# Weighting of matches shared by ScalarE and GpSimd, and four buffers of raw expert rows, in a decoder block with product-key experts

## What is computed

```python
idx = i_top0 * PEER_NKEYS + i_top1            # 8 x 16 experts of a token
act = gelu(einsum("phkd,pd->phk", u_tab[idx], tb))
out = einsum("phk,phkd->pd", g * act, v_tab[idx])
```

## Time and profile before

| | |
|---|---|
| median of 3 runs | 2198.37 us (2197.58 to 2199.71) |
| profiled execution | 2195.7 us |
| its span, first to last instruction | 2193.9 us |
| granted TensorE clock, mean | 0.981 |
| TensorE / VectorE / ScalarE / GpSimd busy | 94% / 80% / 37% / 36% of the span |
| first table with spreading | 1097 to 1613 us |
| rest of the first table | 1613 to 1655 us |
| second table | 1655 to 2182 us |

### The profile page before, as it was taken

One profiled execution on the slowest core, in us unless ns is written; L12 is line 12 of the kernel. 1 busy time (PEld: TensorE's weight loads), 2 busy tenths in 40 slices (PEclk: granted clock), 3 DMA queues, 4 the chain that ended last, 5 costly groups with the idle time before them and its releaser, 6 DMA issues. The chain is left out here.

```text
span 2193.9 us, 35121 instructions
## 1 busy us (share of the span) xinstructions
PE 2069.3 (94%) x11175; PEld 1812.6 (83%) x11175; DVE 1748.5 (80%) x3357; ACT 816.6 (37%) x1350; POOL 798.8 (36%) x673
## 2 busy tenths in 40 slices
PE   6998988979999998999899999999999999999997
PEld 5886788758888877889799999999997888888886
DVE  3776655677768845999799999999988888888887
ACT  4454423522322223344443443344333333333333
POOL 2000044500000000325488989888963222222221
PEclk9999999989999999999999999999999999999999
DMA  6743100405234215224489999999899999999995
GB/s 136 93 61 39 20 1 20 135 13 139 70 91 117 79 62 178 68 73 153 143 284 300 325 333 320 318 323 322 278 362 373 338 337 337 338 337 336 341 335 198
DMA packets 296052, 445.77 MB, mean 203 GB/s; under 512 B 84612, under 2 KB 221988, under 8 KB 295716
## 3 DMA queue, kind: packets, MB, share of 16 engines
q1 hardware_dynamic: 239348, 273.26, 41.9%
q0 software_dynamic: 41472, 151.01, 19.7%
q10 hardware_dynamic: 15152, 20.51, 2.5%
HBM read 398.05 MB, written 46.14 MB: 202 GB/s over the span
## 5 line engine op out<-in xcount | busy, mean ns | idle before, releaser
L2278 PE MATMUL bank<-u_hi,u_one 128*128 128x512 f32 x768 | 299.7, 390 | 3.6 <-DVE u_two L2426 3.6
L2278 PE MATMUL bank<-u_lo,u_one 128*128 128x512 f32 x768 | 299.3, 390 | 0.0
L2278 PE MATMUL bank<-u_hi,u_two 128*128 128x512 f32 x768 | 299.2, 390 | 0.0
L2261 PE MATMUL bank<-xt_hi,u_hi 128*128 128x352 f32 x832 | 277.9, 334 | 0.7 <-DVE u_lo L2316 0.7
L1997 POOL DMA_INDIRECT row_slot<-in_peer_v_dram,row_index x128 | 141.1, 1102 | 377.1 <-DVE row_x L2434 362.6
L2261 PE MATMUL bank<-xt_lo,u_hi 128*128 128x352 f32 x832 | 269.1, 323 | 0.0
L2261 PE MATMUL bank<-xt_hi,u_lo 128*128 128x352 f32 x832 | 268.9, 323 | 0.0
L2499 ACT ACTIVATE u_hi<-xh 128x1024 fp32r<-128x1024 f32 x128 | 135.8, 1061 | 334.9 <-PE bank L2278 331.4
L2423 DVE TENSOR_TENSOR u_lo<-xh,u_hi 128x1024 fp32r<-128x1024 f32 x128 | 156.9, 1226 | 81.2 <-ACT u_hi L2499 81.1
L2190 POOL TENSOR_TENSOR u_two<-u_match,u_weight_hi 128x512 fp32r<-128x512 f32 x96 | 179.9, 1874 | 31.2 <-DVE u_match L2324 30.5
L1517 PE MATMUL bank<-xt_hi,x_whi 128*128 128x512 f32 x448 | 177.8, 397 | 1.6 <-DVE xt_lo L181 0.9
(11 more groups left out here) (464 smaller groups left out, 5024.7 us busy)
## 6 DMA issues: line engine op xcount, KB each, us to landing
xh<-in_peer_v_dram SPq DMA_DIRECT2D x128, 512.0 KB, 5.5
xh<-in_peer_u_dram SPq DMA_DIRECT2D x104, 512.0 KB, 6.3
x_raw<-in_w_in_dram SPq DMA_DIRECT2D x56, 512.0 KB, 6.9
acts<-xh ACTq DMA_DIRECT2D x102, 192.0 KB, 5.2
weights<-u_spread SPq DMA_DIRECT2D x32, 512.0 KB, 9.8
v_gg<-weights SPq DMA_DIRECT2D x128, 128.0 KB, 5.3
p_raw<-in_w_in_dram SPq DMA_DIRECT2D x12, 1024.0 KB, 10.0
q_raw<-in_peer_u_dram SPq DMA_DIRECT2D x24, 512.0 KB, 3.7
```

Source lines behind the costliest of these rows:

```text
L2261: mm = pe.matmul(k.ps[4 + b][:, 0:DOTTED], w[b][:, c, :], x[:, c, 0:DOTTED], start=(c == 0 and w is uhi and x is hi), stop=(c == DC - 1 an ...
L2278: mm = pe.matmul(k.ps[q][:, :], h[b][:, t * P:(t + 1) * P], w[b][:, f], start=start and h is hhi and w is vhi, stop=stop and h is hlo, ski ...
```

## The change

- GpSimd's `weigh` makes the low product only, counted by a new semaphore `low_done`. A new `weigh` on ScalarE makes the high product, as four copies of 128x128 with a scale per partition, for step s+1, between the high parts of tile s+1 and the Gelu of tile s. The weight tiles are four columns wider, so that a step behind the last has zeros.
- VectorE's two comparisons are parted: `matches` comes first in the step, ahead of the low parts, and waits for both products of the step before; `onehot` stays where it was.
- Raw rows have four buffers: two in `xh`, and the first two quarters of the residual's tile. Load i+4 waits until tile i is turned. The other two quarters of the residual are loaded at i = 96 as before, the first two after the last loads of the second table; the additions wait for them.
- Pieces of a chunk are stored in iterations 1, 2, 4, 6, 8, 10, 12 and 13 of the next chunk, not 0, 2, ... 14.
- ScalarE waits for the split of the gathered weights at the start of the last chunk.
- In the second table the first loads into `xh` 2 and 3 wait for one turn less.

```diff
@@ -1980,6 +1980,7 @@
+STORE_AT = (1, 2, 4, 6, 8, 10, 12, 13)
@@ -2015,15 +2016,16 @@
-        raw = [k.xh[:, 2 + b, :] for b in range(2)]
 ...
-        weight_hi = k.sb("u_weight_hi", [P, DENSE], F32R, ctx=st)
-        weight_lo = k.sb("u_weight_lo", [P, DENSE], ctx=st)
+        weight_hi = k.sb("u_weight_hi", [P, DENSE + TOK_TILE], F32R, ctx=st)
+        weight_lo = k.sb("u_weight_lo", [P, DENSE + TOK_TILE], ctx=st)
 ...
-        names = ("raw_in", "turned", "hi_done", "lo_done", "product", "ga_done", "ga_out")
+        raw_in = k.sems("u_raw_in", PER)
+        low_done = k.sem("u_low_done")
+        names = ("turned", "hi_done", "lo_done", "product", "ga_done", "ga_out")
@@ -2073,11 +2075,12 @@
-        last_ga = [match[:, :, :].rearrange("p q n -> p (q n)")[:, 0:DENSE], weight_lo[:, :]]
+        last_ga = [match[:, :, :].rearrange("p q n -> p (q n)")[:, 0:DENSE], weight_lo[:, 0:DENSE]]
 ...
+        raw = [k.xh[:, 2, :], k.xh[:, 3, :], rest[:, 0, :], rest[:, 1, :]]
@@ -2101,12 +2104,11 @@
-                def load(n, u):
-
-                    b, before = place(n, u)
-                    sp.wait_ge(s["turned"][b], after(before * 2))
-                    sp.dma_start(raw[b], u_dram[:, bass.ds((n * PER + (u + EARLY)) % EXPERT_TILES, 1), :].rearrange("p a d -> p (a d)")
-                                 ).then_inc(s["raw_in"][b], 16)
+                def load(i):
+
+                    if i >= PER:
+                        sp.wait_ge(s["turned"][i % 2], after((i - PER) // 2 * 2 + 2))
+                    sp.dma_start(raw[i % PER], u_dram[:, (i + EARLY) % EXPERT_TILES, :]).then_inc(raw_in[i % PER], 16)
@@ -2123,14 +2125,16 @@
+                for i in range(2, PER):
+                    load(i)
                 for i in range(tiles):
-                    if i + 2 < tiles:
-                        load(i // PER, i % PER + 2)
-                    c, piece = i // CHUNK_STEPS - 1, i % CHUNK_STEPS // 2
-                    if 0 <= c < STORED and i % 2 == 0:
-                        store(c, piece)
+                    if i + PER < tiles:
+                        load(i + PER)
+                    c, at = i // CHUNK_STEPS - 1, i % CHUNK_STEPS
+                    if 0 <= c < STORED and at in STORE_AT:
+                        store(c, STORE_AT.index(at))
                     if i == steps:
-                        sp.dma_start(rest[:, :, :], residual).then_inc(res_in, 16)
+                        sp.dma_start(rest[:, 2:TT, :], residual[:, 2:TT, :]).then_inc(res_in, 16)
@@ -2148,7 +2152,7 @@
-                        sp.wait_ge(s["turned"][u - 2], after(2 * uses))
+                        sp.wait_ge(s["turned"][u - 2], after(2 * uses - 2))
@@ -2166,6 +2170,9 @@
+                for b in range(2):
+                    sp.wait_ge(s["turned"][b], after(2 * uses))
+                sp.dma_start(rest[:, 0:2, :], residual[:, 0:2, :]).then_inc(res_in, 16)
@@ -2186,9 +2193,8 @@
-                    for h, part in enumerate((weight_hi[:, tok].bitcast(F32), weight_lo[:, tok])):
-                        pool.tensor_tensor(two[b][:, :, h, :], match[:, :, :], part.unsqueeze(2).to_broadcast([P, TOK_TILE, P]),
-                                           ALU.mult).then_inc(two_done, 1)
+                    pool.tensor_tensor(two[b][:, :, 1, :], match[:, :, :], weight_lo[:, tok].unsqueeze(2).to_broadcast([P, TOK_TILE, P]),
+                                       ALU.mult).then_inc(low_done, 1)
@@ -2235,16 +2241,17 @@
-                    pe.wait_ge(s["raw_in"][b], after(before * 16))
+                    pe.wait_ge(raw_in[u % PER], after((n + u // PER) * 16 + (16 if u % PER >= 2 else 0)))
 ...
-                            mm = pe.transpose(k.ps[2 * b + f][:, c % 4 * P:(c % 4 + 1) * P], raw[b][:, c * P:(c + 1) * P], k.ident[:, :])
+                            mm = pe.transpose(k.ps[2 * b + f][:, c % 4 * P:(c % 4 + 1) * P], raw[u % PER][:, c * P:(c + 1) * P], k.ident[:, :])
 ...
-                    pe.wait_ge(two_done, after(step * 2 + 2))
+                    pe.wait_ge(two_done, after(step + 1))
+                    pe.wait_ge(low_done, after(step + 1))
@@ -2316,12 +2323,15 @@
-                def onehots(at, b):
-
-                    keys = k.row[:, :].unsqueeze(1).to_broadcast([P, TOK_TILE, P])
-                    picks = lambda n: chosen[:, n, at].unsqueeze(2).to_broadcast([P, TOK_TILE, P])
-                    dve.tensor_tensor(one[b][:, :, :], keys, picks(0), ALU.is_equal).then_inc(one_done, 1)
-                    dve.tensor_tensor(match[:, :, :], keys, picks(1), ALU.is_equal).then_inc(match_done, 1)
+                keys = k.row[:, :].unsqueeze(1).to_broadcast([P, TOK_TILE, P])
+
+                def onehot(at, b):
+                    dve.tensor_tensor(one[b][:, :, :], keys, chosen[:, 0, at].unsqueeze(2).to_broadcast([P, TOK_TILE, P]), ALU.is_equal
+                                      ).then_inc(one_done, 1)
+
+                def matches(at):
+                    dve.tensor_tensor(match[:, :, :], keys, chosen[:, 1, at].unsqueeze(2).to_broadcast([P, TOK_TILE, P]), ALU.is_equal
+                                      ).then_inc(match_done, 1)
@@ -2358,19 +2368,23 @@
+                        if c is not None:
+                            step = n * PER + u
+                            dve.wait_ge(two_done, after(step + 1))
+                            dve.wait_ge(low_done, after(step + 1))
+                            matches(bass.ds(step * TOK_TILE + TOK_TILE, TOK_TILE))
 ...
-                            step = n * PER + u
                             dve.wait_ge(spread_ready, after(step))
-                            dve.wait_ge(two_done, after(step * 2 + 2))
-                            onehots(bass.ds(step * TOK_TILE + TOK_TILE, TOK_TILE), (u + 1) % 2)
+                            onehot(bass.ds(step * TOK_TILE + TOK_TILE, TOK_TILE), (u + 1) % 2)
 ...
-                        dve.wait_ge(two_done, after(2 * steps))
+                        dve.wait_ge(two_done, after(steps + 1))
+                        dve.wait_ge(low_done, after(steps))
@@ -2382,13 +2396,15 @@
-                dve.tensor_copy(weight_hi[:, :], chosen[:, 2, 0:DENSE]).then_inc(weight_split, 1)
+                dve.memset(chosen[:, :, DENSE:DENSE + TOK_TILE], 0.0).then_inc(weight_split, 1)
                 dve.wait_ge(weight_split, after(1))
-                dve.tensor_tensor(weight_lo[:, :], chosen[:, 2, 0:DENSE], weight_hi[:, :].bitcast(F32), ALU.subtract).then_inc(weight_split, 1)
-                dve.memset(chosen[:, :, DENSE:DENSE + TOK_TILE], 0.0).then_inc(weight_split, 1)
+                dve.tensor_copy(weight_hi[:, :], chosen[:, 2, :]).then_inc(weight_split, 1)
+                dve.wait_ge(weight_split, after(2))
+                dve.tensor_tensor(weight_lo[:, :], chosen[:, 2, :], weight_hi[:, :].bitcast(F32), ALU.subtract).then_inc(weight_split, 1)
 ...
-                onehots(slice(0, TOK_TILE), 0)
+                matches(slice(0, TOK_TILE))
+                onehot(slice(0, TOK_TILE), 0)
@@ -2448,6 +2464,7 @@
+                    dve.wait_ge(res_in, 32 if t < 2 else 16)
@@ -2485,6 +2502,15 @@
+                def weigh(step, b):
+                    act.wait_ge(match_done, after(step + 1))
+                    act.wait_ge(spread_ready, after(step - 1) if not isinstance(step, int) else max(step, 1))
+                    for q in range(TOK_TILE):
+                        at = bass.ds(step * TOK_TILE + q, 1) if not isinstance(step, int) else slice(step * TOK_TILE + q, step * TOK_TILE + q + 1)
+                        for h, part in ((0, weight_hi[:, at].bitcast(F32)),):
+                            ins = act.activation(two[b][:, q, h, :], match[:, q, :], ACT.Copy, scale=part)
+                    ins.then_inc(two_done, 1)
+
@@ -2507,13 +2533,14 @@
+                        if c is not None:
+                            weigh(n * PER + (u + 1), (u + 1) % 2)
 ...
-                            act.wait_ge(match_done, after(steps + 1))
-                            act.wait_ge(two_done, after(2 * steps))
+                            act.wait_ge(two_done, after(steps + 1))
@@ -2527,10 +2554,14 @@
+                    if c == CHUNKS - 1:
+                        act.wait_ge(weight_split, after(5))
 ...
+                act.wait_ge(weight_split, after(3))
+                weigh(0, 0)
 ...
```

## The result

| | before | after |
|---|---|---|
| median of the runs | 2198.61 us (4 runs, 2197.58 to 2199.71) | **2176.47 us** (4 runs, 2173.27 to 2178.45) |
| ratio to before | | 0.9898, 95% interval 0.9881 to 0.9915 |
| profiled execution, its span | 2195.7, 2193.9 | 2176.06, 2174.3 |
| mean granted clock | 0.981 | 0.981 |

Two runs further down that took 2954.83 and 4205.35 us, where all others of their kernels lie within 6 us, are left out of every number.

A forecast was written before the change was run, and what follows sets the result against it. GpSimd's multiplications and late loads were taken to hold the expert-tile stage above TensorE's pace. Stage -25.9, start -1.0 and end of tiles -1.9 sum to -28.8 us, from 2198.4 to 2169.6; range 2164 to 2184.

The forecast's parts named there:

- The stage on TensorE's pace: Expert-tile stage: GpSimd's multiplications and late loads cost 26.4 us over TensorE's own pace; the change saves 25.9 there.
- the floor of 5.154: Expert-tile stage: us per spread step when TensorE has nothing to wait for, against 5.43 before.
- the change takes no work from TensorE: Expert-tile stage: TensorE's work stays the same, so the 26.4 us lost to something else is the whole prize.
- the second table is otherwise untouched: Second-table stage: the same instruction by instruction, with no term in the sum.
- 6.9 with waits: GpSimd in the expert-tile stage: about 6.9 us stay per two steps, down from 10.68, against 10.31 on TensorE.
- 9.6 us per two steps forecast: VectorE in the expert-tile stage: falls from 10.43 us to 9.6 per two steps, against 10.31 on TensorE.
- The 0.84: VectorE per two steps: 0.84 us of a dot product and GpSimd's multiplication excluding each other, claimed to go.
- rival B: Expert-tile stage: GpSimd's low multiplication meets VectorE's dots every step, 5.64 us each, total 2215.5 us; chance 0.06.
- Loads: Raw expert tiles: four buffers and later stores together remove the transposes' load waits, 23.0 us in 12 places.
- Start, last chunk, end of the tiles: Around the stage: start -1.0 us, ScalarE's wait for weights at the last chunk +0.5, eight tiles without spread -1.9.
- A: Transfers bind and load waits stay: 2181.1 us if half of the 23.0 stays, 2192.6 if all; chance 0.12.
- C: ScalarE bounds the stage, by copies at 0.74 us or a late wait for matches: 2193, at half 2181; chance 0.06.

## Why the prediction was right, and where it was short

**The stage on TensorE's pace: right.** Chain on TensorE alone (from 1300 to 1345 us), no wait on a load and dots of 1.21 to 1.23 us throughout the stage. With the operands' distance kept, the floor of 5.154 is met to a nanosecond (5.153), and the whole kernel takes 2168.5 us against the 2169.6 forecast. That the kernel as it was changed lands in the range too, 6.9 us above the forecast, is in part luck: its range had no room set aside for what follows, and 32 bytes instead of 64 would have put it far outside.

**The step that failed: "the change takes no work from TensorE" and "the second table is otherwise untouched".** The instructions are, their operands' places aren't. Two tiles four columns wider move u_hi and u_lo by 64 bytes, and each product on them costs 1% more: 4.1 us in the second table, 4.0 in the stage, some 0.3 in the eight tiles behind it. I read the diff for its instructions and not for the layout behind a widened tile. No row of before could have given the price, but that a tile moved was to be seen.

**GpSimd: right.** It has 271.37 us of work in 493, 5.7 us per two steps where I had put 6.9 with waits.

**ScalarE: right.** I took 368 ns for a copy; one takes 391 on average, but they overlap, so that four in a row are 1.28 us against 1.5. The estimate from the Trainium skill (ScalarE: Activation LUTs, What ACT_TABLE_LOAD costs) was 1.2; the trace agrees. The work is hidden: the wait ahead of the Gelu is 0.96 us a step still. How well it hides depends on the order of VectorE's work, which I had priced only by the exclusion.

**VectorE: 9.6 us per two steps forecast, 10.24 measured** (486.72 us in the 490 us of the kernel with old distances, 95.1 steps). The 0.84 did go from the dots, and 0.67 came back on the one-hot: its mean is 1028 ns in the stage, 692 before. This is the wider rule of the Trainium skill (SBUF — State Buffer, Who interferes with whom), by which a comparison with both inputs in SBUF is excluded too; the trace agrees (0.68 us alone, 1.40 beside GpSimd). So the step "the 0.84 goes too, and VectorE falls to 9.6" did not hold: one hit in two steps stayed, as rival B has it. It cost nothing only because 10.24 is just under TensorE's 10.31. I had left 0.7 us of room and 0.07 is left, and that it was enough is luck.

**Loads: right.** The prediction says that GpSimd's lag and the load waits overlap, and takes both at once. The trace shows the overlap: the weighting alone brings the load waits from 25.8 to 11.0 us. By medians the stores alone give 5.9 us, stores with buffers 11.4, the weighting alone 20.0, and all of it 28.3; the sum of the last two parts, 31.4, is 3.1 more than the whole, which is not clear of the noise. What I had as two parts that act "together" need not both be there: the four buffers alone would have done.

**Start, last chunk, end of the tiles.** From the transposes of the two tiles turned ahead of the stage to the stage's first ones it is 10.34 us after, 11.21 before: -0.9 against -1.0. The new wait at the last chunk is there (2.0 us, once), but no transposes come late by it: 0 instead of 0.5. The end gained 2.7 us instead of 1.9; the wait for the first weighted tile is 2.48 us, 0.24 shorter, the rest came from between the tiles.

**The rivals.** Of A nothing: with a DMA share of 0.98 in the stage no transpose waited. C: no wait of TensorE on a high part. B and C are what the order of matches holds off: without it their mechanisms, the exclusion and a ScalarE that is late for want of matches, cost 66 us. That is far more than the 46 us between my B and my forecast, because, as the timeline above shows, ScalarE's queue passes the delay on.

## What to carry to other kernels

Read a diff for the addresses that it moves as well as for its instructions: where products bind, compare their spacing in a stage that the change should not touch, and pin the operands' places before judging the rest. Where three engines are nearly full, hand work to the one whose queue has a wait in it, and put the producer of that work first on its own engine, because everything in order behind the taker waits with it. Price parts of a change one by one in experiments, not by adding up their waits: here one of two cures for the late loads was enough.

## What the runs showed of the hardware that was not expected

- The pace of TensorE's products depends on where their operands lie in SBUF: for 128x512 products 226.7 ns at the old distance, 228.9 with u_hi and u_lo moved by +64 bytes, 232.4 at +128, 233.3 at -64 and at +32 (one run each). With both operands moved by 64 it was 226.7 again, so that it seems to be the distance between them. The rule is open.
- An indirect load's issue on GpSimd is stretched beside a dot too: 1.72 us where a dot ran when it began (1311.51; the dot ended at 1312.30, and from there it is the usual 0.94), 0.98 where none did (1317.52). It is so throughout the stage of the kernel after: 1.71 to 1.72 us for all 47 that began while a dot ran, 0.94 to 1.13 for the 95 others, of which 45 began beside the comparison for `match`.
- A multiplication on GpSimd costs VectorE's one-hot comparison 0.72 us when both run at once (1.40 against 0.68), nearly as much as it costs a dot (0.84).
